# Three RMS norms between the stages of a transformer kernel: whole sums by ones, roots by Ln and Exp on ScalarE, two norms in one factor

## The chip, the core and the metric

The kernel runs on one core of a Trainium2 chip, on TensorE (PE in the profile), VectorE (DVE), ScalarE (ACT), GpSimd (POOL) and SyncE (SP, which only issues DMAs here). The metric is the device time of one execution in microseconds, the median of several.

## The reference, cut to what matters

512 tokens of width 1024 go through a first block (two layers, each a norm, an attention and a SwiGLU feed-forward part, and a norm of the output) and a second block (a gated mixer of two convolutions, a SwiGLU part, and a norm of the output).

```python
def _rmsnorm(h, g):
    y = h * lax.rsqrt(jnp.mean(h * h, axis=-1, keepdims=True) + 1e-6)
    return y * g
...
    x = _rmsnorm(h, norm_final)                       # end of the first block
    mod = jax.nn.silu(c) @ w_ada + b_ada
    sh1, sc1, g1, sh2, sc2, g2 = jnp.split(mod[:, None, :], 6, axis=-1)
    h = rms_norm(x, norm_mix_g) * (1.0 + sc1) + sh1   # the mixer's input
...
    x = x + g1 * mix
    h2 = rms_norm(x, norm_ffn_g) * (1.0 + sc2) + sh2  # the last feed-forward part
    a, b = jnp.split(h2 @ w_ffn_in, 2, axis=-1)
    x = x + g2 * ((jax.nn.silu(a) * b) @ w_ffn_out)
    return rms_norm(x, final_norm_g)                  # the output
```

## The kernel before, in words

**Layout.** Everything is kept transposed: the stream `h` is [128, 8, 512], channels on the partitions in KD = 8 tiles and tokens along the row. Each tensor that a product reads is split into a high and a low part, both in a rounded float32 (`xh`, `xl`, or `yh`, `yl`). Weights come as a stream of [128, 8, 128] units, two (s = 0, 1) to a step u. ScalarE makes the high part of a weight (`split_hi`, L336), VectorE the low part (`split_lo`, L616), and in the conv stage POOL does (L1173). `product` on TensorE then issues, for each of 8 k, three matmuls of 512 columns into PSUM bank G[s]: L1218, L1219 and L1220. `both` interleaves two such products by k, so that they can follow tiles as they come. The weight of a slot is split for the next step when its product is done; loads wait for the split before them.

**Order.** Every engine has its own program, written out by hand, and semaphores tie them. ScalarE, VectorE, POOL and SP work in order. A feed-forward part is done in three parts of 8, 8 and 6 hidden tiles, each followed by a `residual` of 8 products, which are added to `h` (L630, or with a gate L632). In the residual ScalarE also squares each finished tile into `sq[s]` (L343), and POOL adds it to `ssum` (L1063). At the end of the first block ScalarE squares each tile a second time with the gain of the output norm (`gains_sq`, L361, into `tmp[s]`), and POOL adds it to `ssum2` (L1072).

**A norm, before.** TensorE multiplies four blocks of `ssum` by one column of ones (`statistic`, L1239), which puts the sums of 512 tokens on 128 partitions in four columns of bank O. VectorE makes mean plus eps (L650), POOL raises it to -0.5 (`inverse_root`, L1077), VectorE writes the roots on diagonals (L652), and TensorE spreads these over all partitions by a product with ones (`spread_root`, L1245). VectorE copies the bank to `rstd` (L658).

**Between the blocks** two norms come one after another, the output's (S_FIN) and that of the mixer's input (S_MIX2). Both sums are taken at once. VectorE works out the second mean from the second sum and the first root (L901 to L910), the diagonals are made at L893, and `output` scales the eight tiles of `h` by the output norm (L898), four before and four behind the second diagonal. Only then is the second factor copied (L922).

**`modulated`** makes the operand of the next products from `h`. VectorE scales two tiles into `tmp[0]` and `tmp[1]` (L826), ScalarE adds the shift and rounds them (L514), and VectorE makes the low parts (L832), two tiles at a time. TensorE's `both` follows by `x_lo`. This is done between the blocks and ahead of the last feed-forward part.

**After `modulated` between the blocks** comes the conv stage (`conf`): per pair of products VectorE multiplies a gated tile (L936) and does about eight taps of a 31-tap convolution (L848), with its sums in PSUM banks Z[0] and Z[1]. Later steps use Z[2] too.

**The end.** After the last residual the norm's chain runs, VectorE scales eight tiles (L1049), and SP stores each as it is done (L324).

Of the kernel before, what the change touches and what calls it, by code (L numbers as in the profile page):

```python
# [27 lines left out]
P = 128  # L28
# [114 lines left out]
def build_program(nc, x_t, const_d, vec_d, stream, ada_w, out_t):  # L143
    with ExitStack() as ctx:
# [25 lines left out]
        mean4 = sb("mean4", [P, NB])  # L170
        gmc = sb("gmc", [P, 16])
        mhalf = sb("mhalf", [P, 1])
# [45 lines left out]
        sum2_ready = sem("sum2_ready")  # L218
# [3 lines left out]
        rstd_ready = sem("rstd_ready")  # L222
        mod_t = sem("mod_t")
        x_hi, x_lo = sem("x_hi"), sem("x_lo")
# [24 lines left out]
        done, stored = sem("done"), sem("stored")  # L249
# [22 lines left out]
        S_IN, S_FFN0, S_MID, S_FFN1, S_FIN, S_MIX2, S_MEAN, S_VAR, S_FFN2, S_OUT = range(10)  # L272
# [3 lines left out]
        def _(eng):  # L276
# [52 lines left out]
        def _(eng):  # L329
# [15 lines left out]
            def residual(u0, rnd, gains=None, gains2=None, gains_sq=None, last=False):  # L345

                def pair(u):
                    for s in range(2):
# [9 lines left out]
                        square(n, s, 8 * rnd + n, h, evac[s], u + 1)  # L358
                        if gains_sq is not None:
                            wait_apart(eng, sq2_added, n + 1, passed)  # L360
                            eng.activation(tmp[s][:, :], tile(h, n), ACT.Square,  # L361
                                           scale=col(vec, gains_sq + n)).then_inc(sq2_ready, 1)
                with eng.Fori(u0, u0 + KD // 2 - last) as u:
                    pair(u)
                if last:
                    pair(u0 + KD // 2 - 1)

# [141 lines left out]
            def modulated(shift, dst, before):  # L509
                with eng.Fori(0, KD // 2) as i:  # L510
                    for s in range(2):
                        n = 2 * i + s
                        wait_apart(eng, mod_t, n + before + 1, passed)
                        eng.activation(tile(dst, n), tmp[s][:, :], ACT.Identity,  # L514
                                       bias=col(modc, shift + n)).then_inc(x_hi, 1)
# [17 lines left out]
            ffn(1, yh, lambda u: residual(u, Q_FIN, gains_sq=V_FIN))  # L533
            modulated(M_SH1, xh, 0)
# [63 lines left out]
            with eng.Fori(U_CO, U_CO + KD // 2) as u:  # L598
                for s in range(2):
# [3 lines left out]
                    eng.activation(tile(xh, n), tmp[s][:, :], ACT.Copy).then_inc(mix_hi, 1)  # L603
            residual(U_OUT, Q_FFN2)
            modulated(M_SH2, yh, KD)
            ffn(2, xh, lambda u: residual(u, Q_OUT, last=True))


        @block.vector
        def _(eng):  # L610
# [209 lines left out]
            def modulated(gm, shift, hi, lo, before, x_before):  # L820

                with eng.Fori(0, KD // 2) as i:
                    for s in range(2):
                        n = 2 * i + s
                        eng.wait_ge(x_lo, n + x_before - 1)
                        eng.scalar_tensor_tensor(tmp[s][:, :], tile(h, n), col(gmc, gm + n), rstd[:, :], ALU.mult,  # L826
                                                 ALU.mult).then_inc(mod_t, 1)
                    for s in range(2):
                        n = 2 * i + s
                        eng.wait_ge(x_hi, n + x_before + 1)  # L830
                        eng.wait_ge(mod_t, n + before + 1)
                        eng.scalar_tensor_tensor(tile(lo, n), tmp[s][:, :], col(modc, shift + n), f32(tile(hi, n)),  # L832
                                                 ALU.add, ALU.subtract).then_inc(x_lo, 1)
# [39 lines left out]
            half = ADA_TILES  # L873
            eng.wait_ge(ada_mm, half)
# [718 lines left out]
```

## Time and profile before

| what | value |
|---|---|
| median of 3 runs | 2182.43 us (2182.33 to 2182.46) |
| the profiled execution, its own time | 2180.67 us |
| its span in the trace | 2178.6 us |
| mean granted clock of TensorE | 0.983 |
| busy: PE, DVE, ACT, POOL | 96%, 51%, 38%, 35% |
| DMA over the span | 214.24 MB, mean 98 GB/s |

Times in the trace are counted from the span's start. The granted clock is 1.00 at TensorE's upper level (2.4 GHz) and 0.50 at the lower (1.2 GHz). "Idle before" in a timeline row stands in brackets with what ended it.

### The profile page before, as it was taken

Reading aid. Unit: us, or ns where it says so; the run is one execution under the profiler, and the core shown is the slowest. Engines: PE = TensorE matmul, PEld = TensorE weight load, DVE = VectorE, ACT = ScalarE, POOL = GpSimd, SP = SyncE. Lnnn points to the kernel's source line nnn. Section 1 sums busy time; section 2 is a strip of 40 time slices with the busy share of each in tenths; the row PEclk is TensorE's granted clock in tenths of the full one; section 3 lists DMA queues with packets and bytes.
Section 4 is the critical chain, followed back from the end, with each engine's and each line's share of the span. In section 5 each row is a group of like instructions: output and inputs, shape, how many; then the busy total and the mean of one; then the engine's idle time right before and its main releaser. Section 6 shows DMA issues by size and latency. Waiting matters only on the chain.

```text
span 2178.6 us, 30020 instructions
## 1 busy us (share of the span) xinstructions
PE 2091.0 (96%) x9676; PEld 1691.8 (78%) x9676; DVE 1103.5 (51%) x1441; ACT 824.5 (38%) x1120; POOL 752.4 (35%) x522
## 2 busy tenths in 40 slices
PE   7999999999999999999999997999999989999997
PEld 5877788888887777788888875888887767888885
DVE  5444444444356666545454445589855443332324
ACT  5555445222244444454222243422225225422222
POOL 3111156864034333267862142444443021101012
PEclk9999999999999999999999997999999999999998
DMA  3111134443232111243533231222322222222222
GB/s 139 59 58 58 56 128 145 164 145 116 97 106 78 58 58 59 70 142 125 192 136 105 95 112 44 97 96 96 96 96 78 91 83 77 96 96 96 97 96 97
DMA packets 59663, 214.24 MB, mean 98 GB/s; under 512 B 6624, under 2 KB 6752, under 8 KB 59488
## 3 DMA queue, kind: packets, MB, share of 16 engines
q1 hardware_dynamic: 59616, 213.63, 29.2%
q8 instruction: 27, 0.44, 0.1%
q14 instruction: 20, 0.16, 0.0%
HBM read 211.51 MB, written 2.10 MB: 98 GB/s over the span
## 4 chain that ended last, share of the span: by engine, by line
PE 89%; DVE 3%; issue 3%; POOL 2%; ACT 2%; DMA 1%; DVEq 0%; SPq 0%; POOLq 0%; ACTq 0%
PE G L1218 27%; PE G L1220 27%; PE G L1219 27%; PE Z L1315 2%; PE O L1371 2%; PE Z L1302 1%; PE Z L1350 1%; DVE wl L616 1%; DMA raw<-stream 1%; ACT wh L336 1%; POOL ssum L1063 1%; DVE ez L731 1%; PE O L1239 0%; PE O L1245 0%; PE Z L1389 0%
## 5 line engine op out<-in xcount | busy, mean ns | idle before, releaser
L336 ACT ACTIVATE wh<-raw 128x1024 fp32r<-128x1024 f32 x348 | 369.4, 1061 | 978.5 <-PE G L1220 912.7
L1218 PE MATMUL G<-xh,wh 128*128 128x512 f32 x1648 | 655.3, 398 | 26.7 <-DVE xl L621 9.0
L1220 PE MATMUL G<-xh,wl 128*128 128x512 f32 x1648 | 646.0, 392 | 0.0
L1219 PE MATMUL G<-xl,wh 128*128 128x512 f32 x1648 | 645.6, 392 | 0.0
L616 DVE TENSOR_TENSOR wl<-raw,wh 128x1024 fp32r<-128x1024 f32 x292 | 437.0, 1496 | 216.2 <-ACT wh L336 212.6
L1218 PE MATMUL G<-yh,wh 128*128 128x512 f32 x960 | 379.4, 395 | 16.4 <-DVE wl L616 10.4
L1218 PEld LDWEIGHTS G<-xh,wh 128*128 128x128 f32 x1648 | 311.9, 189 | 104.6 <-issue 23.8
L1220 PE MATMUL G<-yh,wl 128*128 128x512 f32 x960 | 375.7, 391 | 0.0
L1219 PE MATMUL G<-yl,wh 128*128 128x512 f32 x960 | 375.7, 391 | 0.0
L1220 PEld LDWEIGHTS G<-xh,wl 128*128 128x128 f32 x1648 | 311.7, 189 | 66.8
L1219 PEld LDWEIGHTS G<-xl,wh 128*128 128x128 f32 x1648 | 312.3, 189 | 63.4 <-issue 0.7
L1218 PEld LDWEIGHTS G<-yh,wh 128*128 128x128 f32 x960 | 181.4, 189 | 61.2 <-DVE wl L616 13.0
L1220 PEld LDWEIGHTS G<-yh,wl 128*128 128x128 f32 x960 | 181.3, 189 | 38.4
L1219 PEld LDWEIGHTS G<-yl,wh 128*128 128x128 f32 x960 | 181.5, 189 | 36.8 <-issue 0.2
L1173 POOL TENSOR_TENSOR wl<-raw,wh 128x1024 fp32r<-128x1024 f32 x56 | 135.8, 2424 | 192.9 <-ACT wh L336 192.9
L1063 POOL TENSOR_TENSOR ssum<-ssum,sq 128x512 f32<-128x512 f32 x64 | 95.3, 1488 | 285.4 <-ACT sq L343 283.8
L848 DVE SCALAR_TENSOR_TENSOR Z<-cin,vec,Z 128x512 f32<-128x512 f32 x224 | 151.7, 748 | 0.0
L1149 POOL TENSOR_TENSOR xl<-csb,xh 128x512 f32 x22 | 36.3, 1651 | 306.3 <-ACT xh L499 306.3
L1143 POOL TENSOR_TENSOR af<-si,us 128x512 f32<-128x512 f32 x44 | 56.7, 1289 | 240.2 <-DVE us L803 236.7
L1126 POOL TENSOR_TENSOR aprod<-aprod 128x512 f32<-128x512 f32 x96 | 134.4, 1400 | 7.5
L630 DVE TENSOR_TENSOR h<-G,h 128x512 f32 x64 | 44.2, 691 | 124.4 <-PE G L1220 124.4
L1122 POOL TENSOR_TENSOR aprod<-araw,cs 128x1024 f32<-128x1024 f32 x48 | 92.0, 1917 | 1.7 <-POOL ssum L1057 0.3
(170 smaller groups left out, 1909.0 us busy)
## 6 DMA issues: line engine op xcount, KB each, us to landing
raw<-stream SPq DMA_DIRECT2D x348, 512.0 KB, 3.3
araw<-ada_w SPq DMA_DIRECT2D x48, 512.0 KB, 4.0
h<-x_t SPq DMA_DIRECT2D x8, 256.0 KB, 7.2
out_t<-h SPq DMA_DIRECT2D x8, 256.0 KB, 2.2
con<-const_d SPq DMA_DIRECT2D x1, 1536.0 KB, 10.3
vec<-vec_d SPq DMA_DIRECT2D x1, 212.0 KB, 2.5
```

What stands on the lines that cost most here:

```text
L336: eng.activation(wh[s][:, :, :], raw[s][:, :, :], ACT.Copy).then_inc(w_hi, 1)
L616: eng.tensor_tensor(wl[s][:, :, :], raw[s][:, :, :], f32(wh[s][:, :, :]), ALU.subtract).then_inc(w_lo, 1)
L630: eng.tensor_tensor(tile(h, n), G[s][:, :], tile(h, n), ALU.add).then_inc(evac[s], 1)
L848: eng.scalar_tensor_tensor(tile(acc, t) if k == CONF_K - 2 else total, window, weight, total, ALU.mult, ALU.add).then_inc(tap_d, 1)
L1063: eng.tensor_tensor(ssum[:, :], ssum[:, :], sq[s][:, :], ALU.add).then_inc(sq_added, 1)
L1122: eng.tensor_tensor(aprod[:, :, :], araw[s][:, :, :], cs[:, :].unsqueeze(2).to_broadcast([P, KD, P]), ALU.mult).then_inc(ada_fold, 1)
L1126: eng.tensor_tensor(aprod[:, 0:half, :], aprod[:, 0:half, :], aprod[:, half:2 * half, :], ALU.add).then_inc(ada_fold, 1)
L1143: eng.tensor_tensor(af[:, :], si[:, :], us[:, :], ALU.mult).then_inc(a_raw, 1)
L1173: eng.tensor_tensor(wl[s][:, :, :], raw[s][:, :, :], f32(wh[s][:, :, :]), ALU.subtract).then_inc(w_lo, 1)
L1218: eng.matmul(G[s][:, :], wh[s][:, k, :], src_h[:, k, :], start=k == 0, stop=False)
L1219: eng.matmul(G[s][:, :], wh[s][:, k, :], src_l[:, k, :], start=False, stop=False)
L1220: mm = eng.matmul(G[s][:, :], wl[s][:, k, :], src_h[:, k, :], start=False, stop=k == kt - 1)
```

## The change

**Sums.** In three places (between the blocks, ahead of the last feed-forward part, at the end) POOL adds only the squares of tiles 0 to 6. TensorE multiplies that sum of [128, 512] by a full block of ones (`wide_sum`, first part), and as soon as ScalarE has the square of tile 7 it adds a like product of it in the same bank. Every partition then has all 512 sums. The two norms between the blocks use banks O and WF = Z[3]; their first parts are issued ahead of their last parts.

**Roots.** ScalarE takes Ln with eps as bias, and Exp with -0.5 as scale, back into the bank. For this it loads the table set of Ln and Exp ahead of three residuals. The four-column chain, the diagonals and the copies to `rstd` are gone in these places; the other norms keep them.

**Two norms in one factor.** The second norm's input is the first one's output, so the factor for `h` is the inverse root of mean(h² (g² + eps)) + eps². The tiles are squared with the gain sqrt(g² + eps) (`gfe`, made from the gains by VectorE and POOL well before), the mixer's gain `gmc` is multiplied by the output gain, and this square is done ahead of the plain one. The eight scalings by the output norm are no longer between the norms: `output(n)` stands in `conf`, behind the taps of each pair.

**`modulated`.** VectorE scales tiles into PSUM banks (even tiles Z[0] and Z[2], odd ones Z[1]). Even tiles: ScalarE makes the high part and VectorE the low part, out of the bank. Odd tiles: ScalarE writes the shifted tile to `tmp[1]` and copies it to the high part, and POOL subtracts. The loop is written out.

**The end.** ScalarE stores `h` times the output gain for tiles 0 to 5 during the last residual (`acc`). VectorE scales tiles 3 to 7, and POOL multiplies tiles 0 to 2 of `acc` by a second copy of the factor. The stores are issued in the order 3, 0, 4, 1, 5, 2, 6, 7.

The small products that make `modc` and `gmc` move from behind the last residual of the first block to ahead of it.

```diff
+        S_IN, S_FFN0, S_MID, S_FFN1, S_MEAN, S_VAR = range(6)
+        W_MIX2, W_FIN, W_FFN2, W_OUT = range(4)
+        POOL_OUT = 3
+        WF = Z[3]
@@ SyncE, the stores @@
-            for n in range(KD):
-                eng.wait_ge(done, n + 1)
+            for n in (3, 0, 4, 1, 5, 2, 6, 7):
+                if n < POOL_OUT:
+                    eng.wait_ge(done_p, n + 1)
+                else:
+                    eng.wait_ge(done_d, n - POOL_OUT + 1)
@@ ScalarE, in residual @@
-                        square(n, s, 8 * rnd + n, h, evac[s], u + 1)
-                        if gains_sq is not None:
+                        if fin:
                             wait_apart(eng, sq2_added, n + 1, passed)
                             eng.activation(tmp[s][:, :], tile(h, n), ACT.Square,
-                                           scale=col(vec, gains_sq + n)).then_inc(sq2_ready, 1)
+                                           scale=col(gfe, n)).then_inc(sq2_ready, 1)
+                        square(n, s, 8 * rnd + n, h, evac[s], u + 1)
+                        if store_gain:
+                            eng.activation(tile(acc, n), tile(h, n), ACT.Copy,
+                                           scale=col(vec, V_FIN2 + n)).then_inc(hg_ready, 1)
...
+            def inverse_root(idx, total, out, eps, between):
+                eng.wait_ge(wide, idx + 1)
+                eng.activation(between[:, :], total[:, :], ACT.Ln, bias=epsc[:, eps:eps + 1],
+                               scale=1.0 / D).then_inc(wide_ln, 1)
+                eng.wait_ge(wide_ln, idx + 1)
+                eng.activation(out[:, :], between[:, :], ACT.Exp, scale=-0.5).then_inc(wide_rstd, 1)
...
-                        eng.activation(tile(dst, n), tmp[s][:, :], ACT.Identity,
-                                       bias=col(modc, shift + n)).then_inc(x_hi, 1)
+                r = KD // 2 * rnd
+                for i in range(KD // 2):
+                    n = 2 * i
+                    eng.wait_ge(mod_t, 2 * (r + i) + 1)
+                    eng.activation(hi[:, n, :], Z[n % 4][:, :], ACT.Identity,
+                                   bias=modc[:, shift + n:shift + n + 1]).then_inc(mod_hi0, 1)
+                    eng.wait_ge(mod_t, 2 * (r + i) + 2)
+                    wait(eng, mod_lo[1], r + i)
+                    eng.activation(tmp[1][:, :], Z[1][:, :], ACT.Identity,
+                                   bias=modc[:, shift + n + 1:shift + n + 2]).then_inc(mod_x1, 1)
+                    eng.wait_ge(mod_x1, r + i + 1)
+                    eng.activation(hi[:, n + 1, :], tmp[1][:, :], ACT.Copy).then_inc(mod_hi1, 1)
...
-            ffn(1, yh, lambda u: residual(u, Q_FIN, gains_sq=V_FIN))
-            modulated(M_SH1, xh, 0)
+            def last_of_first(u):
+                eng.preload_act_table_set("natural_log_exp_and_others")
+                eng.wait_ge(gfe_ready, 1)
+                residual(u, Q_FIN, fin=True)
+            ffn(1, yh, last_of_first)
+            inverse_root(W_MIX2, O, O, 1, rstd)
+            inverse_root(W_FIN, WF, WF, 0, csb)
+            modulated(0, M_SH1, xh)
...
+            eng.preload_act_table_set("natural_log_exp_and_others")
             residual(U_OUT, Q_FFN2)
-            modulated(M_SH2, yh, KD)
-            ffn(2, xh, lambda u: residual(u, Q_OUT, last=True))
+            inverse_root(W_FFN2, O, O, 0, rstd)
+            modulated(1, M_SH2, yh)
+            def last_of_second(u):
+                eng.preload_act_table_set("natural_log_exp_and_others")
+                residual(u, Q_OUT, last=True)
+            ffn(2, xh, last_of_second)
+            inverse_root(W_OUT, O, O, 0, rstd)
+            eng.activation(tmp[0][:, :], rstd[:, :], ACT.Exp, scale=-0.5).then_inc(wide_out, 1)
@@ VectorE, modulated @@
+                def scaled(bank, n):
+                    eng.scalar_tensor_tensor(bank[:, :], h[:, n, :], gmc[:, gm + n:gm + n + 1], O[:, :], ALU.mult,
+                                             ALU.mult).then_inc(mod_t, 1)
+                def even_lo(i):
+                    n = 2 * i
+                    eng.wait_ge(mod_hi0, r + i + 1)
+                    eng.scalar_tensor_tensor(lo[:, n, :], Z[n % 4][:, :], modc[:, shift + n:shift + n + 1],
+                                             f32(hi[:, n, :]), ALU.add, ALU.subtract).then_inc(mod_lo[0], 1)
+                for i in range(KD // 2):
+                    wait(eng, mod_lo[0], r + i - 1)
+                    scaled(Z[2 * i % 4], 2 * i)
+                    if i > 0:
+                        even_lo(i - 1)
+                    wait(eng, mod_x1, r + i)
+                    scaled(Z[1], 2 * i + 1)
+                even_lo(KD // 2 - 1)
...
             def output(n):
-                eng.scalar_tensor_tensor(h[:, n, :], h[:, n, :], vec[:, V_FIN + n:V_FIN + n + 1], rstd[:, :],
+                eng.scalar_tensor_tensor(tile(h, n), tile(h, n), col(vec, V_FIN + n), WF[:, :],
                                          ALU.mult, ALU.mult).then_inc(y_ready, 1)
...
+            eng.wait_ge(gmc_ready, 3)
+            eng.wait_ge(wide_rstd, W_MIX2 + 1)
+            modulated(0, 0, M_SH1, xh, xl)
+            eng.wait_ge(wide_rstd, W_FIN + 1)
             eng.wait_ge(padded, 2)
...
                     taps(t, m, 4)
+                    output(n)
...
+            eng.wait_ge(wide_rstd, W_OUT + 1)
+            for n in range(POOL_OUT, KD):
+                eng.scalar_tensor_tensor(h[:, n, :], h[:, n, :], vec[:, V_FIN2 + n:V_FIN2 + n + 1], O[:, :],
+                                         ALU.mult, ALU.mult).then_inc(done_d, 1)
@@ GpSimd @@
+            def clear_after(idx, rnd):
+                eng.wait_ge(wide, idx + 1)
+                eng.wait_ge(sq_added, 8 * rnd + KD - 1)
+                eng.memset(ssum[:, :], 0.0).then_inc(sq_added, 1)
+            def modulated(rnd, hi, lo):
+                r = KD // 2 * rnd
+                for i in range(KD // 2):
+                    n = 2 * i + 1
+                    eng.wait_ge(mod_hi1, r + i + 1)
+                    eng.tensor_tensor(lo[:, n, :], tmp[1][:, :], f32(hi[:, n, :]), ALU.subtract).then_inc(mod_lo[1], 1)
...
+            for n in range(POOL_OUT):
+                eng.wait_ge(hg_ready, n + 1)
+                eng.wait_ge(wide_out, 1)
+                eng.tensor_tensor(h[:, n, :], acc[:, n, :], tmp[0][:, :], ALU.mult).then_inc(done_p, 1)
@@ TensorE @@
+            def wide_sum(out, first, count, total, last, ready, value, start=True, finish=True):
+                if start:
+                    eng.wait_ge(first, count)
+                    eng.matmul(out[:, :], ones, total, start=True, stop=False)
+                if finish:
+                    eng.wait_ge(ready, value)
+                    eng.matmul(out[:, :], ones, last[:, :], start=False, stop=True).then_inc(wide, 1)
...
-            statistic(sq_added, KD * (Q_FIN + 1))
-            statistic(sq2_added, KD + 2, ssum2, NB)
-            spread_root(S_FIN)
-            spread_root(S_MIX2)
+            mix2 = (O, sq2_added, KD + 1, ssum2, tmp[1], sq2_ready, KD)
+            fin = (WF, sq_added, KD * Q_FIN + KD - 1, ssum[:, :], sq[1], sq_ready, KD * (Q_FIN + 1))
+            wide_sum(*mix2, finish=False)
+            wide_sum(*fin, finish=False)
+            wide_sum(*mix2, start=False)
+            wide_sum(*fin, start=False)
...
-            statistic(sq_added, KD * (Q_FFN2 + 1))
-            spread_root(S_FFN2)
-            ffn(2, yh, yl, xh, xl, 5 * KD)
-            statistic(sq_added, KD * (Q_OUT + 1))
-            spread_root(S_OUT)
+            wide_sum(O, sq_added, KD * Q_FFN2 + KD - 1, ssum[:, :], sq[1], sq_ready, KD * (Q_FFN2 + 1))
+            ffn(2, yh, yl, xh, xl, KD, ready=mod_lo)
+            wide_sum(O, sq_added, KD * Q_OUT + KD - 1, ssum[:, :], sq[1], sq_ready, KD * (Q_OUT + 1))
```


## Rows read from the trace of the kernel before

**Rows 1.** The page: busy time, and the clock in 40 slices

```profile
PE 2091.0 (96%) x9676; PEld 1691.8 (78%) x9676; DVE 1103.5 (51%) x1441; ACT 824.5 (38%) x1120; POOL 752.4 (35%) x522
...
PEclk9999999999999999999999997999999999999998
```

**Rows 2.** Windows of TensorE: us, busy time (instructions), granted clock, DMA share, GB/s

```profile
1302.83:1324.68 21.85, 7.73 (x21) 0.58 0.12 43
1324.68:1330.20 5.52, 5.52 (x13) 0.50 0.00 0
1330.20:1338.42 8.22, 8.22 (x36) 1.00 0.00 0
1341.31:1347.25 5.94, 5.94 (x14) 0.50 0.55 177
1782.35:1794.96 12.61, 3.13 (x11) 0.71 0.13 42
1794.96:1797.70 2.74, 2.74 (x7) 0.50 0.00 0
1797.70:1807.95 10.25, 10.03 (x43) 0.99 0.00 0
1811.35:1814.90 3.55, 3.55 (x10) 0.52 0.64 209
2160.95:2178.60 17.65, 3.94 (x10) 0.56 0.32 119
```

**Rows 3.** Timeline of the first gap: start, us, engine, line, operation, idle before

```profile
1302.21 1.28 POOL L1072 TENSOR_TENSOR con<-con,tmp 128x512 f32<-128x512 f32 x1
...
1303.95 1.23 DVE L616 TENSOR_TENSOR wl<-raw,wh 128x1024 fp32r<-128x1024 f32 x1 [0.27 <-ACT wh L336]
...
1304.10 0.63 ACT L343 ACTIVATE sq<-h 128x512 f32 x1 [0.18 <-issue]
...
1304.63 0.71 ACT L361 ACTIVATE tmp<-h,vec 128x512 f32 x1
...
1312.01 2.07 PE L1245 MATMUL O<-tmp,con 128*128 128x512 f32 x2 [2.08 <-DVE tmp L893]
...
1314.84 2.74 DVE L898 SCALAR_TENSOR_TENSOR h<-h,vec,rstd 128x512 f32<-128x512 f32 x4
```

**Rows 4.** Timeline of TensorE around the sum of the conv's channels

```profile
1635.26 1.02 PE L1509 MATMUL O<-ssum,con 128*128 128x512 f32 x2
```

**Rows 5.** Groups of ScalarE by form: an Exp out of PSUM

```profile
L402 ACT ACTIVATE ez<-Z 128x512 f32<-128x512 f32 x40 | 23.0, 597 | 40.2 <-PE Z L1315 40.2
```

**Rows 6.** Timeline of the second gap

```profile
1783.80 0.63 ACT L343 ACTIVATE sq<-h 128x512 f32 x1 [0.35 <-issue]
...
1793.16 1.44 ACT L514 ACTIVATE yh<-tmp,modc 128x512 f32 x2 [8.74 <-DVE tmp L826]
```

**Rows 7.** Timeline of the tail, and the DMA rate from 2165 to 2179

```profile
2161.79 0.63 ACT L343 ACTIVATE sq<-h 128x512 f32<-128x512 f32 x1 [3.45 <-DVE h L632]
...
2162.50 1.26 POOL L1063 TENSOR_TENSOR ssum<-ssum,sq 128x512 f32<-128x512 f32 x1 [2.71 <-ACT sq L343]
...
2170.59 5.39 DVE L1049 SCALAR_TENSOR_TENSOR h<-h,vec,rstd 128x512 f32<-128x512 f32 x8
...
GB/s 0 0 0 0 0 0 0 0 0 0 0 0 0 0 0 0 0 0 0 0 129 374 375 380 386 363 398 386 386 392 381 386 375 374 381 380 146 0 0 0
```

**Rows 8.** Groups of POOL by form: low parts of the hidden tiles

```profile
L1149 POOL TENSOR_TENSOR xl<-csb,xh 128x512 f32 x22 | 36.3, 1651 | 306.3 <-ACT xh L499 306.3
...
L1145 POOL TENSOR_TENSOR yl<-af,yh 128x512 f32 x42 | 54.2, 1289 | 44.4 <-ACT yh L492 44.4
```

**Rows 9.** Timeline of ScalarE: a load of an activation table

```profile
1334.09 1.28 ACT L336 ACT_TABLE_LOAD   x1
```

**Rows 10.** Timeline of VectorE in a pair of the conv

```profile
1366.18 0.69 DVE L936 TENSOR_TENSOR cin<-G,sgt 128x512 f32<-128x512 f32 x1 [4.92 <-PE G L1220]
...
1366.79 5.36 DVE L848 SCALAR_TENSOR_TENSOR Z<-cin,vec,Z 128x512 f32<-128x512 f32 x8
```

More of the change, by code:

```diff
@@ L343, in square, with residual, pair @@
                 eng.activation(sq[s][:, :], tile(src, n), ACT.Square).then_inc(sq_ready, 1)
-            def residual(u0, rnd, gains=None, gains2=None, gains_sq=None, last=False):
-                def pair(u):
+            def residual(u0, rnd, gains=None, gains2=None, fin=False, last=False):
+                def pair(u, store_gain=False):
                     for s in range(2):
@@ L507, in ffn, with modulated @@
                     u += KD // 2
[L509 to L513, printed above, removed]
-                        eng.activation(tile(dst, n), tmp[s][:, :], ACT.Identity,
-                                       bias=col(modc, shift + n)).then_inc(x_hi, 1)
+            def modulated(rnd, shift, hi):
+                r = KD // 2 * rnd
[10 more added lines that the diff above has]
+                    eng.activation(hi[:, n + 1, :], tmp[1][:, :], ACT.Copy).then_inc(mod_hi1, 1)
             eng.wait_ge(in_vec, 16)
@@ L818, in ffn, with modulated @@
                     u += KD // 2
[L820 to L833, printed above, removed]
+            def modulated(rnd, gm, shift, hi, lo):
+                r = KD // 2 * rnd
[15 more added lines that the diff above has]
+                even_lo(KD // 2 - 1)
             chain = Z
@@ L892, in diagonal, with last_of_first @@
-            def diagonal():
-                eng.tensor_tensor(tmp[0][:, :].rearrange("p (b t) -> p b t", b=NB),
-                                  ident.unsqueeze(1).to_broadcast([P, NB, P]),
-                                  root4[:, :].unsqueeze(2).to_broadcast([P, NB, P]), ALU.mult).then_inc(diag_ready, 1)
+            def last_of_first(u):
+                eng.wait_ge(ada_mm, 2 * half)
+                eng.tensor_tensor(modc[:, half:2 * half], M[:, half:2 * half], vec[:, V_ADA + half:V_ADA + 2 * half],
+                                  ALU.add).then_inc(modc_ready, 1)
+                eng.wait_ge(modc_ready, 2)
+                for at, scale, gain in ((0, M_SC1, V_MIX2), (KD, M_SC2, V_FFN2)):
+                    eng.scalar_tensor_tensor(gmc[:, at:at + KD], modc[:, scale:scale + KD], 1.0, vec[:, gain:gain + KD],
+                                             ALU.add, ALU.mult).then_inc(gmc_ready, 1)
+                eng.wait_ge(gmc_ready, 1)
+                eng.tensor_tensor(gmc[:, 0:KD], gmc[:, 0:KD], vec[:, V_FIN:V_FIN + KD], ALU.mult).then_inc(gmc_ready, 1)
+                residual(u)
@@ L910, in _ @@
-            eng.tensor_scalar(var4[:, :], mean4[:, :], EPS, None, ALU.add).then_inc(var_ready, 1)
-            eng.wait_ge(spread, S_FIN + 1)
-            eng.tensor_copy(rstd[:, :], O[:, :]).then_inc(rstd_ready, 1)
-            eng.wait_ge(rstd_ready, 5)
-            for n in range(KD // 2):
-                output(n)
-            eng.wait_ge(root_ready, S_MIX2 + 1)
-            diagonal()
-            for n in range(KD // 2, KD):
-                output(n)
-            eng.wait_ge(y_ready, KD)
@@ L1166, in ffn @@
                                 fold_ada(2 * w + (j + nt) + s, s)
-                add_round(rnd, second=which == 1)
+                add_round(rnd, second=which == 1, but_last=which > 0)
             def split_lo(u, s):
```

137 lines of the change are left out of this document (66 added, 71 removed).

## The prediction

> **What bounds the kernel now.** I read the page first, then the windows, then the timeline of each gap. The page says TensorE is busy 96% of the span at nearly full clock throughout, with two dips in the clock row, one past the middle and one at the end [rows 1]. So only what shortens TensorE's idle stretches, its low-clock stretches or the tail counts. The windows give the three places that the change touches [rows 2]. First gap: 1302.83 to 1324.68, 21.85 us without a product, then 5.52 us of products at half clock (0.50, the 1.2 GHz level), then full clock to 1338.42, where the pair of products interleaved by k is done. Second gap: 12.61 us up to 1794.96, 2.74 us at half clock, done at 1807.95. Tail: 17.65 us from the last product to the span's end. Full products elsewhere are untouched.
>
> The chain in a gap is the same each time: last square on ScalarE, add on POOL, eight tiny matmuls, mean on VectorE, root on POOL (about 1 us for four columns), diagonal on VectorE, spread on TensorE, copy, and then the modulation. In the first gap one chain follows another, and eight output scalings of 0.67 us stand between them: two lots of four at 2.74 us [rows 3].
>
> **The new chain, step by step.** The f32 sum of 128x512 by ones exists once in the trace: 1.02 us at full clock, a second behind it 0.46 + 0.40 us on [rows 4]; at half clock a like one took 2.07 [rows 3]. I take 1.0, because the clock stays full at the start of a gap: means of 0.58, 0.71 and 0.56 between the levels 1 and 0.5 make 3.5, 5.3 and 2.1 us at full clock of 21.85, 12.61 and 17.65 [rows 2], and the early part of the sum now fills some of that time. The other end is 2.07. Ln has a bias from a column, like L361: 0.71 us. Exp into PSUM has constants: 0.60, like L402 out of PSUM [rows 5]. VectorE's scaling is 0.75 us long, 0.68 apart [rows 3, 7]. ScalarE's modulation is 0.72 [rows 6] and its copy, by the square of that length, 0.63 [rows 6]. A signal between engines costs 0.05 to 0.08 us (a square ending 2162.42, its add starting 2162.50 [rows 7]).
>
> *First gap.* POOL's second add for tile 6 started at 1302.21, behind the first, and took 1.28 us [rows 3]. Swapped, the second sum is ready at about 1302.2 and the first at 1303.6, so TensorE does both early parts by 1304.5. Swapping the two squares makes the one that the mixer needs ready at 1304.8 (0.71 us from 1304.10). Its last part ends at 1305.9; Ln and Exp end at 1307.25. VectorE scales tiles 0, 1 and 2 until 1309.4. ScalarE meanwhile does the output's Ln and Exp until 1308.5, then the high part of tile 0 until 1309.15. VectorE's low part (0.75) ends at 1310.1, and TensorE starts, against 1324.68: 14.6 us earlier. That drops two copies, four tiny steps, one diagonal, one root and eight scalings from the path. The output's factor (0.86 us of TensorE, then 1.2 us of ScalarE) lies beside VectorE's three scalings.
>
> *Supply behind tile 0.* Odd tiles go ScalarE 0.72, ScalarE copy 0.63, POOL subtract 1.29, three signals: a round of 2.8 us per two tiles, because tmp[1] is single. A pair of tiles costs TensorE 12 products of 0.228 us, 2.73 us at full clock, 5.1 at half. In the second gap tile 1 is ready 1.35 us after the start and tile 7 three rounds later, 9.75 us. With the clock path of before TensorE needs tile 7 only 12.99 - 1.37 = 11.6 us after its start [rows 2]. So the round binds only above 3.4 us; the same sum gives 3.45 in the first gap (13.74 in place of 12.99, tile 1 after 2.0). I keep the lengths of before for both, so the whole earlier start is kept.
>
> POOL's subtraction is bounded by 1.29 us (L1145, VectorE idle) and 1.65 (L1149, mean of 22, started beside a VectorE weight split) [rows 8]. I take 1.29: here VectorE has h or the high part in SBUF and its other tensor in PSUM, unlike a weight split. The Trainium skill (GPSIMD Engine Reference, Key points) says that POOL shares its SBUF interfaces with VectorE, in contention with instructions that have two SBUF inputs; by that rule the shorter value holds here. By the longer, the round is 3.15 and still hidden, and the tail alone loses 1.1 us.
>
> *Second gap.* The last product ended at 1782.35, so the early part of the sum is done by 1783.4 beside the evacuation; the last square ends at 1784.43 [rows 6]. Last part 1785.5, Ln 1786.25, Exp 1786.9, three scalings 1789.0 with tile 0's high part inside them, low part 1789.75. Against 1794.96: 5.2 us.
>
> *Tail.* The last square ends at 2162.42; POOL's add for tile 6 came a whole product, 4.08 us, ahead of that for tile 7 (2162.50) and takes 1.3, so it is over [rows 7]. Last part 2163.5, Ln 2164.2, Exp 2164.85, first output tile 2165.65, against 2171.34 (2170.59 + 0.75). The stores ran at 375 to 390 GB/s without a break from there [rows 7], 5.5 us for 2.1 MB, and that stays: 7.25 us from first tile to end gives 2172.9. POOL's three tiles start after a second Exp (2165.4) and come at 2166.7, 2168.0 and 2169.3. The queue order 3, 0, 4, 1, 5, 2 leaves the engines idle about 0.3 us: end 2173.2, 5.4 us earlier. At 1.65 each, 4.3.
>
> *At nothing.* Three table preloads of 1.28 us each [rows 9]: each stands behind the last high part and ahead of a weight split that waits for a whole product (4.08 or 5.44 us), in which ScalarE has some 2.4 us of work; uncovered they would cost 3.8 us together. The Silu reload in the last feed-forward part was there before. The eight output scalings go into the first conv pairs: there VectorE did 0.69 + 5.36 us and idled 4.92 us of each 10.9 us pair [rows 10], so 0.68 fits; uncovered, 5.4 us. The gain copies (0.71 on ScalarE, six tiles) sit in 4.08 us products with 1.1 + 0.6 us of other work. The squared gains and their root on POOL (about 1 us) meet folding that has slack over a pair. VectorE's small gain products leave the gap for the head of the residual, where it waits for a product. POOL's clear (0.5) is over before the first odd tile. Nothing is moved past a weight load on SP's queue.
>
> **Sum.** 14.6 + 5.2 + 5.4 = 25.2 us. The profiled execution took 2180.67 us (span 2178.6), so 2155.5 by it. The median of the runs, 2182.43, is 1.8 higher: 2157.2.
>
> **The clock.** Low stretches differ: 5.52 us after the first gap, 2.74 after the second, though the first gap was the longer [rows 2]. Half clock costs half its length in lost products. So each of the two may shift by 1.4 us either way. A further dip lies behind each pair, where TensorE waits for the next weight split: 5.94 and 3.55 us at 0.50 and 0.52 [rows 2], worth 3.0 and 1.7 us, 4.7 in all if both go. The Trainium skill (TensorE: Matmul & The Clock Gate, What you observe) says that the point of return varies from run to run. By that rule the sum keeps its centre and its end is uncertain by these amounts.
>
> **Rivals.**
> Rival A, *more*: the new gaps are short and the early sums fill them, so the dips behind the pairs vanish too. 25.2 + 4.7 = 29.9: 2152.5. For it: two thirds of the first gap go. Against: TensorE still idles over 4 us twice, and the waits for the next split behind the pairs stay. Chance 0.13.
> Rival B, *less*: covers fail. The preloads (3.8) come into sight, or the last parts run at half clock (1.05 each), or POOL takes 1.65 in the tail (1.1). About 4 us are lost: 2161.2. For: none of the preloads' slack is shown by a row at that very place. Chance 0.19.
> Rival C, *slower*: ScalarE and POOL pass tmp[1] back and forth, and this round becomes the bound of both interleaved pairs. Over 3.4 us each extra microsecond costs three in each gap, six together. The gain is gone at 7.6 us a round, and at 8.4 the kernel is 5 us slower, 2187. For: three engine steps in series on one buffer. Against: every step has a row, and with the longest of them it is 3.15. Chance 0.03.
> Rival D, *the change does not do what it says*: the norm's chain is not what ends the gaps, but the interleaved pair's weights are, and the freed time turns up as a wait for them: no change, 2182. Against: the last split of that pair, which TensorE needs, ran from 1303.95 for 1.23 us [rows 3], five microseconds ahead of the new start. Chance 0.02.
>
> **Numbers.** The forecast has 0.63 and 2157.2. The range takes in A with 1.4 us more, and B with a further 4 us for waits that no row shows: 2151 to 2165. Beyond 0.2% (4.4 us, about what a measurement of this kernel can tell from no change): faster 0.95 (forecast, A, B), same 0.02 (D), slower 0.03 (C).
>
> **What would show it.** Right: TensorE's first product after the first gap 7.3 us after the last one before it (21.85 before), 7.4 after the second gap (12.6), and a tail of 12.3 us (17.65); sums of 1.0 us; odd low parts on POOL of 1.3 us, one every 2.8 to 3.2; in the conv, VectorE idle 4.2 us a pair and TensorE without a wait. Wrong: TensorE waiting for POOL's low parts inside the pairs (C), table loads or late splits at the head of a residual (B), sums of 2 us (B), or a clock row without dips (A).

## The result, and the profile after

| | before | after |
|---|---|---|
| median, us (lowest to highest) | 2182.44 (2182.33 to 2183.98), 4 runs | 2154.09 (2152.55 to 2159.98), 4 runs |
| the profiled execution; its span | 2180.67; 2178.6 | 2154.63; 2152.5 |

The ratio is 0.9874, with a 95% interval of 0.9859 to 0.9889: some 27.5 us are gone. The forecast was 2157.2.

The page of the changed kernel, the lines that answer to [rows 1]:

```profile
PE 2080.5 (97%) x9652; PEld 1683.7 (78%) x9652; DVE 1103.9 (51%) x1418; ACT 841.0 (39%) x1146; POOL 754.5 (35%) x527
...
PEclk9999999999999999999999999999999999999999
```

TensorE does nearly the same work in a shorter span, and both dips of its clock row are gone. The timeline of the first gap in the changed kernel, against [rows 3]:

```profile
1303.19 1.02 PE L1309 MATMUL O<-con 128*128 128x512 f32 x2
...
1305.35 1.13 PE L1312 MATMUL O<-tmp,con 128*128 128x512 f32 x2 [0.16 <-ACT tmp L371]
...
1306.51 0.69 ACT L385 ACTIVATE rstd<-O,epsc 128x512 f32<-128x512 f32 x1 [0.70 <-PE O L1312]
...
1307.23 0.60 ACT L388 ACTIVATE O<-rstd 128x512 f32<-128x512 f32 x1
...
1307.95 2.07 DVE L868 SCALAR_TENSOR_TENSOR Z<-h,gmc,O 128x512 f32<-128x512 f32 x3 [2.25 <-ACT O L388]
...
1309.93 0.75 DVE L874 SCALAR_TENSOR_TENSOR xl<-Z,modc,xh 128x512 fp32r<-128x512 f32 x1
```

The early part of a sum (L1309) runs at once behind the last product, the last part (L1312) behind the square. Ln and Exp follow at 0.69 and 0.60 us, then three scalings and the first low part. TensorE's windows of the changed kernel, against [rows 2] (us, busy time, granted clock, DMA share, GB/s):

```profile
1303.42:1310.82 7.40, 3.75 (x8) 1.00 0.34 120
1310.82:1322.45 11.63, 11.62 (x48) 1.00 0.00 0
1325.32:1330.00 4.68, 4.68 (x14) 0.64 0.44 144
...
1775.09:1778.00 2.91, 2.91 (x7) 0.50 0.00 0
...
2140.20:2152.50 12.30, 1.71 (x4) 0.71 0.46 171
```

In the first gap and its pair the clock stayed full, where before 5.52 us were at half. To compare runs I take four measures from the starts of the product matmuls: the two gaps (last matmul to first), the tail (start of the last matmul to the span's end), and the length of all low stretches from 1272 us on (matmuls some 0.43 us apart in place of 0.23; half of that length is lost).

| | first gap | second gap | tail | low stretches |
|---|---|---|---|---|
| before | 22.24 | 13.00 | 18.07 | 20.1 |
| after | 7.86 | 7.99 | 12.96 | 11.2 |
| gain | 14.4 | 5.0 | 5.1 | 4.4 |

That is 28.9, of which 2.3 came back in the convolution (below) and 0.5 by a later arrival at the first gap (the last product matmul ahead of it starts at 1302.96 against 1302.44). It leaves 26.1 us; the two profiled executions differ by 26.0.

The 0.5 is itself a balance of two things that the prediction does not have. By 72 us the profiled execution of the changed kernel was 2.4 us behind: TensorE ran at half clock for 10.2 us from 29.1 on, against 6.8 us from 29.7 before (windows of TensorE, changed kernel first):

```profile
29.10:39.30 10.20, 7.31 (x14) 0.50 0.32 103
```

```profile
29.70:36.50 6.80, 4.57 (x11) 0.50 0.43 130
```

From 72 us to the first gap it gained 1.9 us. Six steps of the second layer's attention, for example, took 160.6 us in all thirteen traces of the changed kernel and its variants (711.49 to 872.12 in this one), against 161.7 before (709.44 to 871.10). No run says which part of the change makes them shorter.

### The profile page after: what moved, and what is told of

Same layout as the page of the kernel before. It is cut to its first block, busy times and chain, and to the rows that moved or that the text cites. A ratio compares the mean times of both kernels' runs of the same rounds, so it can differ in the third digit from the quotient of the medians.

```text
span 2152.5 us, 29802 instructions
## 1 busy us (share of the span) xinstructions
PE 2080.5 (97%) x9652; PEld 1683.7 (78%) x9652; DVE 1103.9 (51%) x1418; ACT 841.0 (39%) x1146; POOL 754.5 (35%) x527
## 3 DMA queue, kind: packets, MB, share of 16 engines
q1 hardware_dynamic: 59616, 213.63, 29.3%
## 4 chain that ended last, share of the span: by engine, by line
PE 91%; DVE 3%; ACT 2%; POOL 2%; issue 1%; DMA 1%; POOLq 0%; SPq 0%; ACTq 0%; DVEq 0%
PE G L1281 28%; PE G L1282 27%; PE G L1283 27%; PE Z L1387 2%; PE O L1443 2%; PE Z L1374 1%; PE Z L1422 1%; DMA raw<-stream 1%; DVE wl L659 1%; ACT wh L347 1%; DVE ez L774 1%; PE Z L1461 0%; PE O L1452 0%; PE O L1461 0%; POOL ssum L1093 0%
## 5 line engine op out<-in xcount | busy, mean ns | idle before, releaser
L1093 POOL TENSOR_TENSOR ssum<-ssum,sq 128x512 f32<-128x512 f32 x61 | 89.3, 1464 | 266.1 <-ACT sq L354 264.5
## 6 DMA issues: line engine op xcount, KB each, us to landing
con<-const_d SPq DMA_DIRECT2D x1, 1536.0 KB, 10.9
```

What stands on the lines that cost most here:

```text
L1093: eng.tensor_tensor(ssum[:, :], ssum[:, :], sq[s][:, :], ALU.add).then_inc(sq_added, 1)
```

## The experiments

Each is a variant of the changed kernel, except where said. The four measures are of its one profiled execution; the medians are of 4 to 6 runs.

| variant | median (lowest to highest) | first gap | second gap | tail | low |
|---|---|---|---|---|---|
| c0_after | 2155.68 (2153.07 to 2168.31) | 7.86 | 8.00 | 13.0 | 11.2 |
| e1_old_tail | 2163.47 (2156.19 to 2164.73) | 7.86 | 7.99 | 17.3 | 15.6 |
| e2_old_chain | 2164.86 (2159.69 to 2169.22) | 7.87 | 13.60 | 13.0 | 29.3 |
| e3_late_sums | 2162.72 (2159.72 to 2166.17) | 9.64 | 10.59 | 13.9 | 17.1 |
| e4_output_late | 2153.93 (2152.51 to 2155.75) | 7.86 | 7.99 | 13.0 | 15.8 |
| e5_on_path | 2160.05 (2156.61 to 2162.95) | 13.13 | 8.00 | 13.0 | 21.0 |
| e6_hold | 2151.55 (2150.12 to 2152.80) | 7.85 | 7.99 | 13.0 | 4.8 |
| e7_pool0 | 2155.82 (2151.67 to 2158.50) | 7.86 | 8.00 | 12.5 | 15.8 |
| e8_two_buffers | 2159.14 (2151.11 to 2159.52) | 7.87 | 8.00 | 13.0 | 24.7 |
| e9_old_operand | 2155.69 (2149.77 to 2156.92) | 7.68 | 7.47 | 13.0 | 18.5 |
| b2_all | 2144.33 (2143.45 to 2148.46) | 7.86 | 7.99 | 12.5 | 0 |
| b3_old_operand | 2145.78 (2145.11 to 2146.42) | 7.69 | 7.47 | 12.5 | 0 |

The gaps repeat within 0.02 us from variant to variant where they are untouched, while the medians scatter by several us. Two things in the traces go with that, the last column and the arrival at the first gap: it lay at 1300.3 to 1301.9 in the six traces of variants with 6.8 us at half clock near 30 us, and at 1302.8 to 1304.4 in the seven with 10.2. So a part's price is read from its gap, not from the medians.

**The control.** 

> The changed kernel itself, as the control for small differences. Its four times lay between 2152.6 and 2160.0, and the traces of its variants differ by how many stretches of 3 to 6 us at half clock lie behind TensorE's waits. Clock theory: the median is 2154 to 2157 and the spread 5 us or more again. Rival, that the spread was drift of the chip: it is under 1 us within one series.

Six runs spread over 15 us, one of them 10 us above the rest; the kernel of before spread over 6.3 us in the same series. So the scatter is not a drift between series.

**One part undone: the tail, and the chain ahead of the last feed-forward part.**

```diff
-            wide_sum(O, sq_added, KD * Q_OUT + KD - 1, ssum[:, :], sq[1], sq_ready, KD * (Q_OUT + 1))
+            statistic(sq_added, KD * (Q_OUT + 1))
+            spread_root(S_OUT)
```

(and the parts of the other engines; e1 also lets VectorE scale all eight output tiles, without the gain copies; e2 likewise has the old chain for S_FFN2)

> The changed kernel with the norm of the output as before: POOL adds all eight squares, four-column sums, root on POOL, diagonals, spread, copy, and VectorE scales and SP stores the tiles in order. Chain theory: the tail of the trace, from the start of the last product's last matmul to the span's end, goes back from 12.96 us to about 18.1, so the time is 5 us (4.5 to 5.6) above the changed kernel's 2154.1, at 2159.2, and nothing changes ahead of the tail. Rival, that the tail's gain lay in POOL's share of the scalings: the part up to the first output tile would hardly move and the time would rise by under 2 us.

> The changed kernel with the old chain of the norm (four-column sums, POOL's root, diagonals, spread, copy) ahead of the last feed-forward part alone; the new way of making its operand (banks, POOL's low parts) stays. Chain theory: the chain alone is worth 4.9 us (last square to the factor: 7.4 us against 2.5), so the gap goes back from 7.5 us to about 12.5 and the time to about 2159. Rival, that the gain of this place came from the operand's new path: the gap rises by under 1.5 us, 2155.6. The low clock behind the gap may move either by 1.4 us.

The tail rose by 4.3 us and the second gap by 5.6. The timeline of the second gap in e2:

```profile
1776.67 1.87 PE L1301 MATMUL O<-con,ssum 128*128 128x1 f32 x8 [3.56 <-POOL ssum L1092]
...
1780.62 2.07 PE L1316 MATMUL O<-tmp,con 128*128 128x512 f32 x2 [2.08 <-DVE tmp L693]
1782.73 0.69 DVE L699 COPY rstd<-O 128x512 f32<-128x512 f32 x1 [2.17 <-PE O L1316]
```

Here the tiny matmuls ran at half clock, 1.87 us. In e1 and in the second gap of before they took 1.05. That explains 0.8 of the 5.6, and in e1 the 0.8 that is missing to the tail of before, which had 1.87. Since e1 also took back POOL's share of the output, which by itself shortens the tail by 0.5 us (e7 below), the tail's chain alone is worth 4.8 us (17.3 against 12.5). Both chains are priced; the rivals (POOL's share of the output, the operand's new path) are out. Both medians rose by more than was expected, 2163.47 for 2159.2 and 2164.86 for 2159; e1 had 15.6 and e2 29.3 us of low stretches, against 11.2.

**The early parts of the sums.**

```diff
                 if start:
                     eng.wait_ge(first, count)
+                    eng.wait_ge(ready, value)
```

> The changed kernel with both parts of every wide sum issued only when the last square is there, so that TensorE is idle until then. Plain latency theory: each sum ends 0.5 to 0.9 us later in the second gap and the tail and some 1.6 us later in the first gap, 3 us in all: 2157. Clock theory (the early parts keep the clock up): besides that, some of the sums run at half clock (2.07 in place of 1.02 us) and the first gap's products start at half clock again (2.8 us), which they did not in the changed kernel's trace: 2160 to 2163, with a granted clock of 0.5 at the first products behind the first gap.

The first gap rose by 1.8 us, the tail by 0.9, the second gap by 2.6. TensorE's timeline and windows of e3 in the second gap:

```profile
1773.40 2.04 PE L1310 MATMUL O<-ssum,con 128*128 128x512 f32 x2 [2.31 <-ACT sq L354]
...
1775.24 1.80 PE L1313 MATMUL O<-sq,con 128*128 128x512 f32 x2
```

```profile
1314.03:1319.30 5.27, 5.27 (x13) 0.50 0.00 0
1771.10:1781.30 10.20, 3.63 (x4) 0.78 0.16 51
1781.30:1787.00 5.70, 5.70 (x14) 0.50 0.00 0
```

The sums there ran at half clock, and the first gap's products started at half clock, as before the change. So in this one trace the late parts cost twice, by latency and by the clock. The second is not certain per run: in e1, e2, e7, e8 and e9, five of the eight traces with the early parts, a first gap of 7.7 to 7.9 us and nothing else in it, a low stretch of 3.0 to 3.4 us still began 0.6 to 1.6 us after the first gap's end (here 5.3 us, from its end on).

**The output scalings, moved on.**

```diff
-                    output(n)
...
+                    output(n)
```

The call leaves `conf`, where it stood behind `taps(t, m, 4)`, for the gate pairs, behind `taps(t, 2 * m + 1, 6)`.

> The changed kernel with the eight scalings of the stream moved from the first conv pairs (where I had put their cost at nothing) to the gate pairs behind the short convolution. In the changed kernel's trace VectorE's additions of two SBUF tiles in the conv (channel sum, low part of the short convolution) take up to 2.87 us instead of 0.69 because they meet POOL's weight splits, VectorE is 4 us late in the short convolution and TensorE waits 0.78 us twice. Collision theory: with the scalings away, the order in time of before returns, all these take 0.69 us, both waits go, and the time falls by 1.5 to 2.4 us, to about 2152. Rival, that the collisions come from the earlier start of the stage and not from the scalings: they stay, and the time does not move (2154).

This is the step at nothing that failed: the cost of the output scalings. The timeline of the changed kernel in the conv:

```profile
1365.12 0.74 DVE L950 SCALAR_TENSOR_TENSOR h<-h,vec,Z 128x512 f32<-128x512 f32 x1
...
1365.78 0.75 DVE L905 SCALAR_TENSOR_TENSOR acc<-Z,vec,acc 128x512 f32<-128x512 f32 x1
...
1366.49 2.40 POOL L1224 TENSOR_TENSOR wl<-raw,wh 128x1024 fp32r<-128x1024 f32 x1 [3.04 <-ACT wh L347]
...
1366.57 2.87 DVE L908 TENSOR_TENSOR ssum<-ssum,acc 128x512 f32<-128x512 f32 x1
```

The output scaling (L950) pushed VectorE's addition of two SBUF tiles (L908) from just ahead of POOL's weight split to just behind its start, and it ended only after the split, 2.87 us instead of 0.69. Groups of VectorE in the conv, first of the changed kernel, then of e4:

```profile
L1009 DVE TENSOR_TENSOR yl<-sq,yh 128x512 f32 x6 | 11.8, 1969 | 0.0
...
L908 DVE TENSOR_TENSOR ssum<-ssum,acc 128x512 f32<-128x512 f32 x7 | 8.4, 1204 | 0.2
```

```profile
L908 DVE TENSOR_TENSOR ssum<-ssum,acc 128x512 f32<-128x512 f32 x7 | 4.8, 692 | 0.2
...
L1008 DVE TENSOR_TENSOR yl<-sq,yh 128x512 f32 x6 | 4.1, 683 | 0.0
```

Once late, VectorE met the splits again and again in the short convolution, and TensorE waited for it twice. The end of one such wait in the changed kernel:

```profile
1490.64 0.69 DVE L1005 TENSOR_TENSOR sq<-G,sq 128x512 f32<-128x512 f32 x1
...
1491.43 0.47 PE L1281 MATMUL G<-xh,wh 128*128 128x512 f32 x1 [0.78 <-issue]
```

In e4 all these collisions and both waits are gone, and the stretch from the second conv product to the channel sum took 292.55 us against 294.88, with a low stretch of 3.0 us in both: 2.3 us, of which the two waits are 1.9 (the products behind each come 0.94 us later than in e4). The times do not show it. The profiled execution of e4 took 2155.75 us, with 4.6 us more of low stretches than the changed kernel's, and the median, 2153.93, is that of no change, where about 2152 was expected. So the stretch shows the effect, and the time does not.

The Trainium skill (GPSIMD Engine Reference, Key points) names the contention of VectorE instructions with two SBUF inputs and GpSimd; the trace agrees, with 0.69 against 2.87 us. Here it is the later one that waits. In e4, as before the change, VectorE's addition starts ahead of the split and takes its 0.69 us, and the split is the one that is longer, 2.79 us instead of 2.40:

```profile
1475.20 0.69 DVE L908 TENSOR_TENSOR ssum<-ssum,acc 128x512 f32<-128x512 f32 x1
1475.37 2.79 POOL L1224 TENSOR_TENSOR wl<-raw,wh 128x1024 fp32r<-128x1024 f32 x1 [3.04 <-ACT wh L347]
```

TensorE did not wait for this split, so it cost nothing.

**The scalings put back on the path.**

```diff
             eng.wait_ge(wide_rstd, W_MIX2 + 1)
+            for n in range(KD):
+                eng.scalar_tensor_tensor(acc[:, n, :], h[:, n, :], vec[:, V_FIN + n:V_FIN + n + 1], O[:, :],
+                                         ALU.mult, ALU.mult)
```

> The changed kernel with eight scalings of 128x512 on VectorE (h by the output gain and the mixer's factor into a buffer that is not read) between the factor of the mixer's input and the making of its operand, where the output scalings stood before. Chain theory: they lie on the path at 0.67 us each, so the first gap (last matmul to first matmul) grows from 7.86 to 13.3 us and the time by 5.4 us plus up to 2.8 for a low clock behind the longer gap, to 2159.5 to 2162. Rival, that the scalings were hidden in part beside ScalarE and POOL: the gap grows by under 3 us.

The first gap grew by 5.27 us. VectorE's timeline of e5 shows them as one block:

```profile
1305.57 5.36 DVE L955 SCALAR_TENSOR_TENSOR acc<-h,vec,O 128x512 f32<-128x512 f32 x8 [2.25 <-ACT O L388]
```

So of the 14.4 us of the first gap, 5.3 are the scalings. The other 9, by subtraction, are the doubled chain with its copies.

**TensorE kept busy.** Beside the real work, products of a constant by ones go to a bank that nothing reads; `idle(n)` issues n of `eng.matmul(Z[4], ones, con[:, C_COS:C_COS + SEQ])`.

```diff
             wide_sum(*fin, start=False)
+            eng.wait_ge(modc_ready, 2)
+            idle(3)
             both(U_CONF, xh, xl, mod_lo, 0)
+            idle(2)
```

> The changed kernel with f32 products of a constant by ones into an unused bank in TensorE's waits: three in the first gap, four in the second, two behind each interleaved pair (1.0 us each; none is read). Clock theory: what scatters the time (2152.6 to 2160 for the changed kernel) are stretches of 3 to 6 us at half clock behind these waits; with TensorE busy there they go, products start at the same times, the low stretches behind both gaps and both pairs (3.0 + 4.8 us in the changed kernel's trace) are absent, and the time is 2151 to 2153. Rival, that these products get in the way (the first real product waits for the last of them): the gaps grow by up to 1 us each and the time does not fall.

TensorE's windows of e6 behind both gaps and both pairs, and around 1645:

```profile
1309.09:1320.70 11.61, 11.61 (x49) 1.00 0.00 0
1323.62:1330.00 6.38, 6.38 (x28) 1.00 0.50 164
1773.33:1784.80 11.47, 11.47 (x49) 1.00 0.00 0
1787.21:1793.00 5.79, 5.79 (x26) 1.00 0.57 184
1641.52:1648.40 6.88, 6.88 (x21) 0.52 0.22 76
```

No gap moved, the clock stayed full where TensorE was filled and fell where it was not, and the runs lie within 2.7 us of each other. The median is 2.5 us below that of the changed kernel, but the intervals of the two ratios to before overlap (0.9843 to 0.9875, and 0.9859 to 0.9889), and 1.7 of the 3.9 us between the two traces lie ahead of the first gap, where the programs do not differ. So the clock is what e6 shows, more than the time. The Trainium skill (TensorE: Matmul & The Clock Gate, HAM oscillation) says that waits of TensorE let its clock fall; here the trace agrees: with the real work waiting as long as before, the clock stays at 1.00 as long as TensorE has other products in the wait.

**The tail's split, the single buffer, and the operand's path.** e7 sets POOL_OUT to 0, stores the tiles in order and drops the gain copies and the second Exp. e8 uses `csb` in turn with `tmp[1]`. e9 makes both operands as before the change, in `tmp[0]` and `tmp[1]`, with all low parts on VectorE, from the new factor.

> The changed kernel with all eight output tiles scaled by VectorE and stored in order, without POOL's three, the gain copies and the second Exp. Store theory: the tail is bound by the first tile and 5.5 us of stores at 375 to 400 GB/s, so the tail stays at 12.9 us or falls by 0.3 to 0.5, as the DMA's pause of 0.5 us between the first and the second tile in the changed kernel's trace goes. Rival, that VectorE's scalings bound it (eight at 0.68 us are 5.4 us): the tail grows by 1 us or more.

> The changed kernel with two buffers in turn for the odd tiles, so that ScalarE does not wait for POOL. Round theory: in the changed kernel's trace a round of ScalarE and POOL takes 2.81 us against 2.73 of TensorE at full clock, and the first interleaved pair took 11.6 us with small waits against 10.9; with two buffers it takes 10.9 to 11.0 at full clock and the time falls by 0.7 us there, less where the clock is low. Rival, that the waits come from VectorE's even tiles, which wait for ScalarE too: no change.

> The changed kernel with the operand of both interleaved pairs made as before (two tiles at a time in SBUF buffers, all low parts on VectorE), but from the new factor. Chain theory: the operand's new path is worth little at the start, 0.3 us a gap (7.86 and 7.99 become 8.2 and 8.3), and some 0.9 us in each pair where the clock is full, as two tiles come every 3.3 us instead of 2.8 and TensorE needs 2.73 for them; 1 to 2.4 us in all, hidden where the clock is low: 2155 to 2157. Rival, that the operand's path carries a large part of the gain: over 4 us.

e7: the tail fell by 0.5 us. The DMA rates over the tail, of the changed kernel and of e7, show why:

```profile
GB/s 0 0 0 0 0 0 0 0 0 0 0 336 397 345 26 9 354 371 414 388 336 397 388 397 354 371 405 388 388 371 371 405 397 345 388 397 95 0 0 0
```

```profile
GB/s 0 0 0 0 0 0 0 0 0 0 0 273 382 391 355 400 382 373 400 364 373 401 364 392 355 391 410 346 400 401 364 391 364 391 400 255 0 0 0 0
```

The pause behind the first tile is the wait for POOL. POOL's share costs, since the stores bound the tail. e8: POOL's odd tiles came every 1.8 to 2.0 us instead of 2.8. The pair took 12.51 us with 3.2 at half clock, so some 10.9 at full clock, against 11.23 in the changed kernel: 0.3 us, half of what I expected. None of it shows in the medians of e7 and e8 (2155.82 and 2159.14), which scatter by more. e9: both gaps were *shorter* than with the new path, by 0.2 and 0.5 us, where I had expected them 0.3 longer.

**Together.** b2 holds e4, e6, e7 and e8, with four more products into the unused bank, one behind the first gate product's step, two behind the next product, and one behind the pair that starts the conv's output product. b3 is b2 with e9's operand and without e8.

> The changed kernel with all that the runs show to help: the output scalings in the gate pairs, products into an unused bank in TensorE's waits (also behind the first gate product and behind the pair of the conv's output product), two buffers for the odd tiles, and the whole output scaled on VectorE. Theory: the effects add up, since each lies in another stretch: 2.3 us from the scalings, 0.5 from the stores, 0.3 from the buffers, and 2 to 4 us from low stretches that the products into the unused bank still left around 1640 and 1675: 2146 (2145 to 2148), below the 2151.6 of the version with these products alone, with no stretch at half clock behind the first gap. Rival, that low stretches move on to other waits: 2149 or more.

> The kernel of b2_all (outputs late, no low clock, whole output on VectorE) with the operand of both pairs made as before the change, in SBUF buffers with all low parts on VectorE. In e9 that made both gaps shorter by 0.2 and 0.5 us and showed no wait in a pair, but the clock was low there. Theory from e9: the operand's new path is worth nothing even at full clock; gaps 7.7 and 7.5 us, pairs 10.9 to 11.1, time 2143.5 to 2144.3. Rival, my step that the old path feeds two tiles in 3.3 us against TensorE's 2.73: the pairs take 11.8 to 12.3 us and the time is 2145 to 2146.

b2 took 2144.33 us, ratio to before 0.9831 (0.9819 to 0.9844). It had no low stretch, pairs of 10.92 and 10.79 us and a short convolution without a wait. It beats both kernels, the changed one by 11.4 us in the same series, and is a little below the 2145 to 2148 that were expected. Of the 11.1 us between the two traces of that series, 2.5 lie ahead of the first gap, where the programs do not differ, 5.6 are the low stretches (half of 11.2), and the rest the conv, the tail and the first pair. b3 had the shorter gaps of e9 (7.69 and 7.47) and pairs of 11.17 and 11.15, as its rounds are 2.87 us:

```profile
1309.57 1.41 DVE L868 SCALAR_TENSOR_TENSOR xl<-tmp,modc,xh 128x512 fp32r<-128x512 f32 x2 [0.39 <-ACT xh L537]
1310.90 1.40 DVE L862 SCALAR_TENSOR_TENSOR tmp<-h,gmc,O 128x512 f32<-128x512 f32 x2
1312.43 1.42 DVE L868 SCALAR_TENSOR_TENSOR xl<-tmp,modc,xh 128x512 fp32r<-128x512 f32 x2
```

That nets out at 0.1 us. Its median is 1.4 us higher and its ratio to before (0.9828, 0.9815 to 0.9841) the same; the last residual of the first block had started 2.4 us later (1269.34 against 1266.90), in stages that the variants share. All of it was there by 72 us, with 10.2 us at half clock near 30 us against 6.8 in b2; why that differs from run to run was not tried. So b3's time came out as the rival had it, but not by the rival's way: its pairs took 11.2 us, not 11.8 or more.

## Why the prediction was right, and where it was not

- **First gap, 14.6 us.** 14.4 measured. The chain came as summed (sum 1.02, Ln 0.69, Exp 0.60, three scalings, low part 0.75). e5 confirms the scalings' share. The start was 0.2 us late, mostly since TensorE's first product came 0.14 us after the end of the low part (1310.68 to 1310.82), for which the sum had nothing.
- **Second gap, 5.2.** 5.0 measured, and e2 gives nearly all of it to the chain (5.6, of which 0.8 is the half clock).
- **Tail, 5.4.** 5.1 measured; 4.3 in e1, with faster tiny matmuls and without POOL's share. The pause in the stores was 0.5 us where I put 0.3.
- **Sums at 1.0 us.** Right in the changed kernel. The other end came in e3 (2.04), without the early parts.
- **Supply.** The round was 2.81 us as worked out, POOL's subtractions took 1.28 to 1.30 us, the shorter of the two values, and nothing waited long: 11.23 us for the first pair at full clock against 10.9 with two buffers. But e9's expectation took all of the 3.3 us that a round took in the loop of before for what the old path needs. Written out, and with the factor read from the bank, it needs 2.87; no run tells these two apart. e9 and b3 do show that the gain does not need POOL's share. Nor did the old round bind before: the first pair there took 13.35 us with 5.3 at half clock, some 10.7 at full clock.
- **Output scalings at nothing.** Wrong, by 2.3 us (e4). The idle time that I read [rows 10] was there and held them, but I counted room and not what else would be shifted against POOL's splits.
- **Table preloads, gain copies, POOL's root at nothing.** No wait of TensorE beyond those of before appeared there: from the last residual's first product to the first gap it took 33.4 us against 33.5, and from the channel sum to the second gap 146.7 in both. Behind the three preloads ScalarE was idle for another 1.23, 0.59 and 1.59 us, so they were covered. Uncovering them was not tried.
- **The clock.** I kept the low stretches of before in the sum and named the gain of their going as rival A (4.7 us, chance 0.13). A like amount, 4.4 us, came in the profiled execution, though only 2.9 of it behind the two pairs, as A has it: 2.6 more came from the first gap's products, which the sum kept at half clock, and 1.1 were lost behind the second gap, where the low stretch grew. e3 gives a part of that to the early sums, but run by run it comes and goes. B's parts did not show, and C's round stayed at 2.81.
- **How near it came, and luck.** By the profiled execution 2155.5 was forecast and 2154.6 measured. The three places gave 0.7 us less than the sum; 4.4 of the clock and 1.9 in the first block came on top; 2.3 in the conv and 2.4 at the start of the execution went off. The mechanism of the three places is shown, but that the total is so near is luck: four terms that the sum does not have nearly cancel.

## What to carry to other kernels

Price a norm between two matmul stages by its chain from the last square to the first low part: a whole sum by ones with its bulk issued early, and the root on the engine that reads PSUM took 5.0 us off the second gap. Work that is moved into idle time of VectorE must also be checked against what it pushes: an addition of two SBUF tiles that slides under a GpSimd instruction waits for all of it. Where TensorE has to wait a few microseconds, products that nobody reads can be cheaper than the half clock behind the wait: none of the three traces with them had a low stretch behind the waits that they fill, and each of the ten without them had at least two there.

## What I had not expected of the hardware

An addition or subtraction of two SBUF tiles on VectorE that starts just behind a GpSimd instruction on two SBUF tiles ends only behind it: 2.87, 2.33, 2.13 or 1.6 us instead of 0.69, by how far the other was. The other way round GpSimd's is the longer one: its split took 2.50 us where VectorE's addition had started 0.45 us ahead, and 2.78 where it had started 0.17 us ahead, instead of 2.40. Of the changed kernel, runs lay up to 15 us apart, and its two traces have the same gaps to 0.01 us; with TensorE filled in its waits, runs lay within 1.3 us (b3) to 5 us (b2).
